# Image tokens 265 to 511 share the context's feed-forward stream; tokens 0 to 264 get a network of their own

## What is computed

```python
def peer_ffn(h, w_query, sub_keys, down, up):      # 128 of 16384 experts for each token
    ...
    act = jax.nn.gelu(jnp.einsum('td,ted->te', h_blk, down[i_blk]), approximate=False)
    return jnp.einsum('te,ted->td', act * g_blk, up[i_blk])

def _conv_ffn(h, w_up, conv_w, conv_b, w_down):    # w_up (1024, 5632), w_down (2816, 1024)
    u = h @ w_up
    up = jnp.pad(u, ((0, 0), (1, 1), (0, 0)))
    u = up[:, :-2] * conv_w[0] + up[:, 1:-1] * conv_w[1] + up[:, 2:] * conv_w[2] + conv_b
    a, v = jnp.split(u, 2, axis=-1)
    return (jax.nn.silu(a) * v) @ w_down

# second_block, layer 0 (pooling windows 2, 4, 8, 16, centred), then layer 1 (attention)
x = x + g1 * y
x = x + g2 * _conv_ffn(_modulate(_rmsnorm(x, norm_w[i, 1]), sh2, sc2), ...)
ctx_s = ctx_s + cg1 * y_c
ctx_s = ctx_s + cg2 * _conv_ffn(_modulate(_rmsnorm(ctx_s, norm_w[i, 1]), csh2, csc2), ...)
```

## Time and profile before

| | us |
|---|---|
| median of 3 runs | 3847.98 |
| lowest, highest | 3846.4, 3851.97 |
| span of the profiled execution | 3845.2 |
| expert rows, first dot to last sum | 1232 to 2641 |
| pooling and norm of the image, up to the first product | 2641 to 2702 |
| feed-forward 0 | 2702 to 3114 |
| projection | 3114 to 3228 |
| share of the span busy: PE, DVE, ACT, POOL | 86%, 67%, 27%, 31% |

### The profile page before, as it was taken

The page is one execution under the profiler, slowest core; times in us unless marked ns, Lnnn a source line. Parts: engine busy times, 40 slices in busy tenths (PEclk is TensorE's granted clock), DMA queues, the critical chain, the costliest instruction groups (busy, mean ns, idle before and its releaser), DMA issues. The chain is left out here.

```text
span 3845.2 us, 60327 instructions
## 1 busy us (share of the span) xinstructions
PE 3314.6 (86%) x24383; PEld 1965.6 (51%) x24383; DVE 2582.6 (67%) x4953; ACT 1054.5 (27%) x2808; POOL 1184.4 (31%) x1166
## 2 busy tenths in 40 slices
PE   7998899899998877566788877776999998899998
PEld 4556665788865322122333331123788444468863
DVE  3866635787857666687687767555777667557765
ACT  2442222444422322333333332233100013410000
POOL 1024310445411333333333333331444310024432
PEclk8999999999999998688989999988999999999999
DMA  4156620000026999999999999996122431012233
GB/s 180 44 201 240 230 99 22 2 11 3 3 105 215 413 414 418 402 403 416 415 413 416 417 417 408 415 419 244 66 88 77 164 114 45 1 66 88 88 120 142
DMA packets 153040, 811.76 MB, mean 211 GB/s; under 512 B 14018, under 2 KB 33405, under 8 KB 69436
## 3 DMA queue, kind: packets, MB, share of 16 engines
q0 software_dynamic: 76256, 544.79, 34.6%
q1 hardware_dynamic: 75356, 261.02, 18.4%
q10 hardware_dynamic: 1152, 2.10, 0.1%
HBM read 805.76 MB, written 2.10 MB: 210 GB/s over the span
## 5 line engine op out<-in xcount | busy, mean ns | idle before, releaser
L2706 PE MATMUL bank<-row,dg 64*64 64x512 f32 x2920 | 455.6, 710 | 241.9 <-ACT dg L2812 241.7
L2909 DVE CUSTOM_DVE_ANT_0 row<-row,bank 128x1024 f32<-128x1024 f32 x365 | 445.8, 1221 | 280.2 <-DMA row<-in_experts,idxs 253.3
L2978 POOL DMA_INDIRECT row<-in_experts,idxs x365 | 352.0, 964 | 664.5 <-PE bank L2706 621.1
L2706 PEld LDWEIGHTS bank<-row,dg 64*64 64x64 f32 x2920 | 99.4, 147 | 464.9 <-issue 464.0
L104 PE MATMUL bank<-hT,wring 128*128 128x256 f32 (+1 forms) x864 | 286.3, 491 | 3.0 <-ACT sq L899 3.0
L2803 ACT ACTIVATE act<-dots 128x2 f32<-128x2 f32 x256 | 52.0, 203 | 863.3 <-DVE dots L2909 863.2
L2706 PE MATMUL bank<-wring,dg 64*64 64x512 f32 x1176 | 182.5, 700 | 106.6 <-ACT dg L2812 106.5
L2978 POOL DMA_INDIRECT wring<-in_experts,idxs x147 | 142.1, 967 | 351.5 <-PE bank L2706 254.0
L2909 DVE CUSTOM_DVE_ANT_0 wring<-wring,bank 128x1024 f32<-128x1024 f32 x147 | 179.5, 1221 | 101.9 <-DMA wring<-in_experts,idxs 92.5
L104 PEld LDWEIGHTS bank<-hT,wring 128*128 128x128 f32 x864 | 165.5, 193 | 118.6 <-issue 101.2
L3096 PEld LDWEIGHTS bank<-c_hid,wring 128*128 128x128 f32 x704 | 127.9, 202 | 173.1 <-issue 160.2
(11 more groups left out here) (657 smaller groups left out, 6771.3 us busy)
## 6 DMA issues: line engine op xcount, KB each, us to landing
wring<-in_ffn_up SPq DMA_DIRECT2D x66, 1024.0 KB, 6.9
wring<-in_ada_w SPq DMA_DIRECT2D x64, 1024.0 KB, 6.1
wring<-in_ffn_w_down SPq DMA_DIRECT2D x50, 1024.0 KB, 7.0
wring<-in_w_in SPq DMA_DIRECT2D x7, 2048.0 KB, 8.3
wring<-in_peer_w_query SPq DMA_DIRECT2D x8, 1024.0 KB, 25.6
wring<-in_attn_w_qkv SPq DMA_DIRECT2D x3, 2048.0 KB, 8.7
row<-in_experts,idxs POOLq DMA_INDIRECT x365, 11.8
wring<-in_ffn_w_down SPq DMA_DIRECT2D x10, 512.0 KB, 4.4
```

The source lines that it names most:

```text
L2706: ins = e.matmul(ks[t][64 * half:64 * half + 64, :], self.dg[u % 4][p, 0:64], row[p, 1024 + half * 512:1536 + half * 512], start=(x == 0), ...
L2909: e.tensor_tensor_reduce(row, row, P.pairs[0], 1.0, 0.0, MUL, ADD, self.dots[:, g % 2, x:x + 1]).then_inc(*V.up("pg_dot", j))
L2978: e.indirect_dma_start(self.places[r], None, P.i["experts"], bass.IndirectOffsetOnAxis(ap=idu[:, b, j % 128:j % 128 + 1], axis=0)).then_in ...
```

## The change

Feed-forward 0 is split by tokens. Image tokens 256 to 511 are pooled, normed and modulated beside the gathers (steps 207 to 297), as soon as their two blocks have left the expert layer, and join the context's 256 tokens: `s_hid` holds both, and each matmul of the stream now has 512 columns. The stream begins at step 296 and runs at 9/4 matmuls a step: 352 up, 176 down. Of step 512 and later, 42 matmuls are left; they are laid between the pooling of the remaining tokens (`BORDER`). The convolution needs neighbours, so tokens 256 to 264 are computed in both places, and the stream's result is kept from 265 on (`yT[..., 0:9]` is zero). The down product gives channels x tokens, which four transposes turn back (`back_pe`). Tokens 0 to 264 pass through `Tail`: plain products of 266 columns instead of the seven, tiles of 1 MB (up) and 0.7 MB (down) through four quarters of the ring, and the norms for attention of block 5 and of the context inside it. `Ffn` stays as it was for layer 1. A host-side copy of the down weights, `ffn_down`, has the order in which tiles are read.

The diff, cut to its core (`ABOUT` lists for the two image blocks the steps at which they are normed, pooled and turned):

```diff
+    UP, NUM, DEN = 296, 9, 4
+    BORDER = (512, 517, 521, 534)
+    ABOUT = ((3, 219, 278, 284), (2, 266, 282, 288))
...
+        first = lambda m: next(r for r in range(self.UP, 600) if self.count(r) >= m)
+        self.evict = {first(8 * q + 8) + 2: q for q in range(44)}
+        self.conv = {r + 1: q for r, q in self.evict.items()}
+        self.down = {first(352 + 22 * c + 22) + 2: c for c in range(8)}
+        self.back = {first(352 + 22 * c + 33) + 2 if c < 7 else self.BORDER[3] - 1: c for c in range(8)}
...
+    def count(self, r):
+        return max(0, min(528, (r - self.UP + 1) * self.NUM // self.DEN))
...
-        for n in range(34):
+        sy.wait_ge(*P.at("c_d", 3))
+        e.dma_start(self.band, band[:, :, BAND_C:BAND_C + BAND_X]).then_inc(*self.Lb[1].up("x_band"))
+        sy.wait_ge(*P.at("c_turned", 0, 1, 1))
+        e.dma_start(self.xgp, i["pool_scale_2"][0].partition_broadcast(128)).then_inc(*self.Lg[1].up("x_scale"))
+        e.dma_start(self.xbias, i["pool_b_2"][0].partition_broadcast(128)).then_inc(*self.Lo[1].up("x_pool_b"))
+        for n in range(38):
...
-            ins = e.matmul(self.ku[:, j * 256:(j + 1) * 256], w[:, c, j * 128:(j + 1) * 128], self.hid[:, c, :], start=(c == 0), stop=(c == 7))
+        ins = pe.e.matmul(self.ku, w[:, c, j * 128:(j + 1) * 128], self.hid[:, :, c, :], start=(c == 0), stop=(c == 7))
...
-        ins = e.matmul(P.ps("c_down", half, b), self.gT[:, k, b * 128:(b + 1) * 128], w[:, y, :], start=(k == 0), stop=(k == 21))
+        ins = pe.e.matmul(self.kd, self.slots[n % 2][:, y * 128:(y + 1) * 128], self.gT[k], start=(k == 0), stop=(k == 21))
...
+        if k == 10 and c:
+            self.back_pe(pe, c - 1)
...
-        if self.UP <= r < self.UP + 176:
-            self.up_pe(pe, r - self.UP)
+        for s in range(self.count(r - 1), self.count(r)):
+            if s < 352:
+                self.up_pe(pe, *divmod(s, 8))
+            else:
+                self.down_pe(pe, *divmod(s - 352, 22))
...
+        if r in self.evict:
+            q = self.evict[r]
+            ac.wait_ge(*P.at("s_u", q))
+            if q >= 2:
+                ac.wait_ge(*P.at("s_conv", q - 2))
+            e.activation(self.pads[q % 2][:, :, 1:257], P.ps("s_u", q).rearrange("p (a n) -> p a n", a=2), ACT.Copy).then_inc(*A.up("free", "s_u", q))
+        if r - 2 in self.conv:
+            row, p = self.column(self.conv[r - 2])
+            if row == 0:
+                e.activation(self.gT[p], self.gT[p], ACT.Silu).then_inc(*A.up("s_silu", p))
...
-    EARLY = {77: 5, 91: 4, 105: 3}
+    EARLY = {105: 3}
...
 # PoolMix.pe
+        for r in range(at[0], at[1]):
+            P.around.pe(pe, r)
...
-            for b, lo, hi, first, last in BANDS[2:]:
+            for b, lo, hi, first, last in BANDS[4:7]:
...
+        for r in range(at[1], at[2]):
+            P.around.pe(pe, r)
...
-        for b in range(2, 6):
+        for b in (3, 2, 4):
...
+        for r in range(at[2], at[3]):
+            P.around.pe(pe, r)
+        for b in (3, 2):
             P.n01.turn_pe(pe, b)
+        P.n01.few_pe(pe)
...
+class Tail(Stage):
+    CTX = (1, 2, 3, 6, 7)
+    LAST = (10, 13, 14)
...
+    def pe(self, pe):
+        for q in range(44):
+            n, j = divmod(q, 2)
+            k = P.bank(pe, "t_u", q)[:, 0:266]
+            pe.wait_ge(*P.at("t_weight", n))
...
+            mm(e, k, [(w[:, c, j * 128:(j + 1) * 128], self.hid[:, c, :]) for c in range(8)]).then_inc(*T_.up("t_u", q))
...
+            if q == self.CTX[3]:
+                self.ctx_pe(pe)
+            if q == self.LAST[1]:
+                P.n10.turn_pe(pe, 5)
+        for c in range(8):
+            self.down_pe(pe, c)
+        P.qkv.unit_pe(pe, 0)
+        self.back_pe(pe, 7)
+        for u in range(1, P.qkv.ahead):
+            P.qkv.unit_pe(pe, u)
+        for b in (2, 3, 4):
+            P.n10.turn_pe(pe, b)
...
-        self.ffn0 = Ffn(self, 0, True, "n01", "ffn0")
+        self.ffn0 = Tail(self, hbase)
...
-        self.units = [(gi, b) for gi in (2, 0, 1) for b in (0, 1, 2, 4, 3, 5) if gi == 2 or b >= 2]
+        self.units = [(2, 0), (2, 1), (2, 5), (0, 5), (2, 2), (2, 3), (2, 4), (0, 2), (0, 3), (0, 4), (1, 5), (1, 2), (1, 3), (1, 4)]
+        self.ahead, self.w = 4, {}
```

946 lines of the change are left out of this document (613 added, 333 removed).

## The result

| | before | after |
|---|---|---|
| median, us | 3847.19 (3843.84 to 3851.97) | 3783.48 (3776.86 to 3785.07) |
| span of the profiled execution, us | 3845.2 | 3774.9 |
| mean granted clock | 0.940 | 0.952 |

The ratio is 0.9832, 95% interval 0.9818 to 0.9846: 1.7% faster. The profiled execution of the changed kernel was the fastest of its four. Its span stands 70.3 us under that of before, and the time between single instructions says where.

What follows compares the result with a forecast made beforehand. Transfers were taken to bound the expert rows and PE feed-forward 0, with PE taking over beside the rows after the change. Terms -24 + 103.5 + 8 - 164.4 + 5 = -71.9 us gave 3776 us, range 3740 to 3845.

Steps and rivals of the forecast that it cites:

- The bound: Expert rows: transfers set the pace before, PE has 0.76 us free in a 2.84 us step; PE takes over.
- Part 2: Rows 296 to 511, each with 9/4 matmuls of 512 columns: 3.24 us a step, +103.5 us.
- The rule on table loads: Stream's silu passes: the skill's 2.66 us a switch would make 117 us of ACT time; the forecast costed them at nothing.
- The share of DMA: Sign of a right forecast: DMA share under 0.95 from row 296 on.
- The loop: Rival, expert rows: seven row buffers, about 17.2 us around, set the step; 3.65 a step gives 3864 us; chance 0.16.
- Gather issue: Rival, expert rows: VectorE's two-input passes delay POOL's gather descriptions, 0.1 us a step, 3797 us; chance 0.06.
- Part 1: Rows 208 to 295 lose the context's weights: -24 us, bounds 16 to 30 saved.
- Part 3: From row 511 to the first feed-forward product: 69 us against 61.1, +8 us, bounds 62 to 80.
- Part 4: Feed-forward 0 itself, 265 tokens with plain products, PE-bound: 248 us against 412.4, -164.4 us.
- Part 5: Projection, VectorE starting its first unit late: 119 us against 113.7, +5 us, bounds 0 to 10.
- The level: Whole kernel: forecast span 3773.3 us, plus 2.8 carried over from the earlier median's excess over its span, 3776 us.

Runs made afterwards that it cites:

- the unedited run: The changed kernel run once more with no edit; median 3781.73 us, ratio 0.9837 to the kernel before.
- the one with the turns moved: Changed kernel, but in the projection PE turns blocks 2 and 3 behind the second unit and block 4 behind the third; ratio 0.9824.
- the combined one: Changed kernel with ACT's copy and silu moved, pooling a row later, hidden-state turns earlier, first key turn before the fifth unit; median 3759.75 us.

## Why the prediction was right, and where it was not

- **The bound.** That the PE work taken out of feed-forward 0 lands on an engine that had 0.76 us free in a step, and so makes it the bound, held: 98% busy, clock 1.00, and the step followed PE's columns (3.235 with 512, 2.886 at the transfers' pace with 256) and not the bytes.
- **Part 2** gave +102.4 for +103.5, and its working holds where nothing waits: 2.93 and 3.79 against 2.94 and 3.79 read, 3.152 a step. 215 of these are 677.8; PE's waits are 14.8; five sets of four transposes before row 511 (`s_yT`), which I had left out here, some 2.5: 695.1, the unedited run's figure. What failed is the cause of the stalls. I took 0.10 a step for VectorE's convolution with a top-k piece behind it and costed ACT's table loads at nothing. The size was 0.07; but with the table loads gone 10.9 of the 14.8 us went, with two of VectorE's passes gone 3.0. "Up to four scaled rows prepared ahead, some 9 us of cover" was the wrong step: ACT waits in its order for a column that PE has just finished, so its lead at that place is two rows and not four.
- **The rule on table loads.** Each load took 1283 ns, and the next instruction began 0.02 us later (2421.55 and 2423.49 above). The Trainium skill ("ScalarE: Activation LUTs", What ACT_TABLE_LOAD costs) adds a drain of about 1380 ns to this figure, together an estimated 117 us for the 44 switches here. No such gap stands in the trace, and with the loads gone PE's waits fell by 10.9 us; with a row more of lead they fell by 14.3 and the loads stayed.
- **The share of DMA** was the wrong sign to name. I wrote that it would be under 0.95; it was 0.95 to 0.98 while PE set the pace, and 1.01 with the tiles sent twice, PE's work in 300 us being the same.
- **The loop** is at most 16.4 us long; my 17.2 added medians of landings that belong to a full queue, and the loop was not near.
- **Gather issue.** The sign that I had named for this rival, gathers longer than 1 us, does show, and the medians (947 ns, 943 before) hide it. Of the 209 that POOL issued in the changed kernel's stream 23 took 1.08 to 1.47 us. Each of the 23 begins while VectorE runs a pass whose two inputs both lie in SBUF (the second and third of a column's convolution, a product, a norm), and each ends 0.82 us after that pass:

```profile
2043.94 0.75 DVE L3387 SCALAR_TENSOR_TENSOR s_gT<-c_pad,c_fp,s_gT 128x512 f32<-128x512 f32 x1
2044.08 1.43 POOL L2974 DMA_INDIRECT row<-in_experts,idxs  x1 [2.85 <-PE bank L2705]
```

- **Part 1** was mis-sized: 13.5 us instead of 24, below my bounds of 16 to 30. The steps without a stream do run at 2.5 us (from 1850.8 to 1911.7 us PE's row pairs come 5 us apart), but I had costed the pooling of blocks 2 and 3 as PE's spare time. What it costs is VectorE's time and its place in the row loop: in rows 284 to 295 VectorE stands 4.1 and 3.2 us for PE's sums,

```profile
1990.50 1.29 DVE L3372 TENSOR_TENSOR x_Ar<-bank,x_gp 128x512 f32<-128x512 f32 x2 [4.11 <-PE bank L104]
...
2018.59 1.37 DVE L3475 TENSOR_SCALAR s_hid<-bank,x_As,modT 128x128 f32<-128x128 f32 x4 [3.18 <-PE bank L3231]
```

  and dots, gathers and rows behind it stand too. Taking both a row later won 4.3 us of the missing 10. The starts of the rows say where all of it went: counted from the first row, row 280 came 24.9 us earlier than before in the profiled execution and 21.0 in the unedited run, as forecast, but row 290 only 12.6 and 8.5 us. In the 38 us of these ten rows VectorE is busy for 30.9. The first two weight tiles fall there too, 2 MB that I had not counted, but they are not the cause: in the run with each tile sent twice, 4 MB stood ahead of the stream, and the stretch was 797.8 us, the shortest of the ten. What makes up the other 6 us stays open.
- **Part 3** gave +4.4 for +8. My sum had the right pieces; PE did not wait for ACT's copy of down column 6, for which I had 2 us, but 1.5 us for that of column 5 and 0.9 for that of column 7; a set of four transposes took 0.5 us (2738.78 to 2739.28) and not 0.9, the turns 2.5 (2788.46 to 2790.96) and not 4.
- **Part 4** gave -168.8 for -164.4. PE-bound, as said. A transposition stands as one record of 0.109 us in the trace and not as two, as a matmul does: the context's 16, block 5's 8 and the returns' 21 took 4.9 us, where I had 9.9 (a return 0.33 us, 2969.96 to 2970.29, and not 0.66). The 2 us for the start lie ahead of the first product. Against that, 1.7 us went to the clock and 0.6 to the products.
- **Part 5** gave +8.5 for +5, inside its bounds. "VectorE takes its first unit some 35 us after the last feed-forward matmul" is what happened (36.8), but I had not read why: 16.7 us of that are ACT waiting for a buffer behind PE's units. Such a wait can be seen in the program before it runs, by following each buffer's next writer to the instruction that frees it.
- **The level.** The forecast of 3776 is 7.5 us under the median of 3783.48. The stages' sum is 1.6 of it; the rest is that this kernel's median lies 8.6 us above the span of its profiled execution, and I had carried over 2.8 from the one of before.

## What to carry to other kernels

Before moving matmuls beside a transfer-bound loop, read from the engine's order whether the new work adds to the loop's own or overlaps it: here a step was the plain sum, row 1.02 + switch 0.19 + 0.86 a matmul, and the sum held to 0.4%. Judge the room of the transfers by bytes per second against the best stretch of the same kernel, not by their busy share. And where two engines feed each other in order, count how many items of lead the feeding engine has at the very place where it waits for the fed one: one row more there was worth 15 us, and made function-table loads free that otherwise cost 11.

## What I had not expected of the hardware

- **The clock at the start of a busy stretch.** The stream begins after 233 us in which PE was busy 58% of the time at a mean granted clock of 0.81. Its first ten microseconds ran at 1.00 in five traces, at 0.94 in the profiled one of the changed kernel, and at 0.78 to 0.83 in seven. The unedited run and the one with the turns moved have the same program up to there, and had 1.00 and 0.79; in the latter the first four records took 3.78 us and not 1.98, and the stream 698.7 and not 695.1 us with the same waits. The same shows in feed-forward 0, whose first ten microseconds, behind PE waits of 0.9 and 1.7 us, had 0.83 in the changed kernel and 1.00 in the combined one: 243.3 against 241.7 us. A mean between the levels of 1.2 and 2.4 GHz means that part of the stretch ran at the lower. What it costs can be worked out: take from the stream's length PE's waits and (1 - granted clock) x length. In the ten traces whose stream has these matmuls, 680.1 to 712.0 us long, 679.6 to 681.0 us are left. By this working up to 2.2 us went at the stream's start. The rest went 1.7 us at a time (once 3.4) at PE waits of 2.1 to 2.7 us inside the stream, in some executions and not in others: six traces have a wait of 2.2 us between 2115 and 2126 us, and behind it the clock fell in four of them. So such a wait can cost nearly twice its length. A difference of 3 us in one stage can therefore be no edit's doing; PE's waits in the stage tell more than its length.
- **Transfers at 417 GB/s beside a PE at the full clock and 97% busy took nothing from PE**: 1162 matmul records in 300 us with 417 and with 371 GB/s.
